# Repeating a constant product on TensorE while it waits, in a fused RWKV-7, GLA and PEER inference step

## The reference, cut to what matters

```python
def _peer(h, wq, subkeys, u, v):
    ...
        q = (xt @ wq).reshape(PEER_BLOCK, PEER_HEADS, 2, PEER_HALF).astype(f32)
        s = jnp.einsum('thpk,hpnk->thpn', q, subkeys.astype(f32))
    ...
        ue = jnp.take(u, expert, axis=0)
        act = jax.nn.gelu(jnp.einsum('thed,td->the', ue, xt).astype(f32), approximate=False)
        ve = jnp.take(v, expert, axis=0)
        return jnp.einsum('the,thed->td', (gate * act).astype(xt.dtype), ve)

for li in range(DEPTH):
    hm = _rmsnorm(x, norm1_g[li]) * (1.0 + sc1) + sh1      # sc, sh, gt from silu(c) @ ada_w
    x = x + gt1 * mix(hm)                                   # RWKV-7 (li = 0) or GLA (li = 1)
    hc = _rmsnorm(x, norm2_g[li]) * (1.0 + sc2) + sh2
    x = x + gt2 * _peer(hc, ...)
```

## Time and profile before

| | |
|---|---|
| time, median of three runs | 3062.83 us (3052.18 to 3067.35) |
| span of the profiled execution | 3042.5 us; the profile gives no other time for it |
| TensorE busy | 1712.4 us (56%), mean granted clock 0.740 |
| VectorE, GpSimd, ScalarE busy | 1595.7, 1320.5, 276.7 us |
| bytes moved by DMA | 828 MB, mean 272 GB/s |

### The profile page before, as it was taken

The page is one execution under the profiler, slowest core; times in us unless marked ns, Lnnn a source line. Parts: engine busy times, 40 slices in busy tenths (PEclk is TensorE's granted clock), DMA queues, the critical chain, the costliest instruction groups (busy, mean ns, idle before and its releaser), DMA issues.

```text
span 3042.5 us, 23984 instructions
## 1 busy us (share of the span) xinstructions
PE 1712.4 (56%) x8811; PEld 1006.3 (33%) x8811; DVE 1595.7 (52%) x2984; ACT 276.7 (9%) x435; POOL 1320.5 (43%) x1160
## 2 busy tenths in 40 slices
PE   3879656826867454636685656358446574002533
PEld 1469412316845113333263225143223261000100
DVE  4253376575844526868313135865775246984033
ACT  1111000010110010010100100011210010000000
POOL 0000012543623555655322354557656125787774
PEclk7889878866879766667677877779677785556875
DMA  7430576964768897777977889879879669799997
GB/s 267 168 125 1 201 280 207 349 220 138 232 221 298 299 325 259 227 239 234 338 284 261 306 286 332 286 264 381 299 277 373 230 225 319 274 332 391 409 409 318
DMA packets 296703, 827.97 MB, mean 272 GB/s; under 512 B 45950, under 2 KB 57134, under 8 KB 296588
## 3 DMA queue, kind: packets, MB, share of 16 engines
q0 software_dynamic: 165888, 604.05, 55.1%
q1 hardware_dynamic: 120132, 218.02, 20.6%
q10 hardware_dynamic: 10568, 4.38, 0.5%
HBM read 816.05 MB, written 10.31 MB: 272 GB/s over the span
## 4 chain that ended last, share of the span: by engine, by line
PE 34%; DVE 22%; DMA 19%; POOL 13%; issue 7%; ACT 3%; PEld 0%; SPq 0%; ACTq 0%; DVEq 0%; PEldq 0%; POOLq 0%
PE psum L1882 31%; POOL arena L695 9%; DMA arena<-in_peer_v,idx_v 6%; DVE arena L1075 6%; DVE arena L1092 6%; POOL wring L695 5%; DMA wring<-in_ada_w 3%; DMA wring<-in_gla_w_in 2%; DMA wring<-in_rw_w_rkv 2%; PE psum L1892 1%; DVE hc L1075 1%; ACT arena L741 1%; DVE hT L1075 1%; DMA vring<-mod_d 1%; DMA wring<-in_peer_v,idx_u 1%
## 5 line engine op out<-in xcount | busy, mean ns | idle before, releaser
L695 POOL DMA_INDIRECT arena<-in_peer_u,idx_u x476 | 628.1, 1320 | 955.7 <-DVEq L1669 415.2
L1882 PE MATMUL psum<-arena 128*32 128x512 f32 (+7 forms) x3666 | 660.2, 619 | 531.3 <-DMA arena<-in_peer_v,idx_v 216.6
L695 POOL DMA_INDIRECT arena<-in_peer_v,idx_v x428 | 431.6, 1008 | 634.6 <-PE psum L1882 477.3
L1092 DVE CUSTOM_DVE_ANT_0 arena<-arena,hc 128x1024 f32<-128x1024 f32 x476 | 565.0, 1225 | 257.9 <-DMA arena<-in_peer_u,idx_u 220.9
L1882 PEld LDWEIGHTS psum<-arena 128*32 128x32 f32 (+2 forms) x3666 | 328.2, 177 | 818.4 <-issue 609.6
L1882 PE MATMUL psum<-wring,arena 128*32 128x512 f32 (+3 forms) x808 | 231.1, 692 | 85.4 <-DMA wring<-in_peer_v,idx_v 43.9
L1882 PE MATMUL psum<-wring,hT 128*128 128x512 f32 (+1 forms) x480 | 192.2, 560 | 27.5 <-DMA wring<-in_gla_w_in 13.6
L1882 PE MATMUL psum<-hT,wring 128*128 128x128 f32 (+4 forms) x1312 | 181.7, 302 | 9.9 <-ACT arena L741 5.0
L1882 PEld LDWEIGHTS psum<-hT,wring 128*128 128x128 f32 (+1 forms) x1312 | 170.9, 203 | 29.7 <-issue 12.9
L741 ACT ACTIVATE arena<-psum 128x512 f32<-128x512 f32 (+6 forms) x125 | 96.7, 774 | 876.8 <-PE psum L1882 644.0
L1882 PEld LDWEIGHTS psum<-wring,arena 128*128 128x128 f32 (+2 forms) x808 | 89.0, 171 | 218.5 <-issue 198.3
(11 more groups left out here) (222 smaller groups left out, 1790.1 us busy)
## 6 DMA issues: line engine op xcount, KB each, us to landing
wring<-in_ada_w SPq DMA_DIRECT2D x24, 2048.0 KB
wring<-in_peer_wq SPq DMA_DIRECT2D x20, 2048.0 KB
wring<-in_rw_w_rkv SPq DMA_DIRECT2D x12, 2048.0 KB
wring<-in_gla_w_in SPq DMA_DIRECT2D x12, 2048.0 KB
wring<-in_rw_wo SPq DMA_DIRECT2D x6, 2048.0 KB
vring<-mod_d SPq DMA_DIRECT2D x22, 512.0 KB
wring<-in_gla_wo SPq DMA_DIRECT2D x4, 2048.0 KB
arena<-in_peer_u,idx_u POOLq DMA_INDIRECT x476, 6.1
```

The source lines that it names most:

```text
L695: pool.indirect_dma_start(slot(s, n), None, v_rows if side else u_rows, bass.IndirectOffsetOnAxis(index, 0)).then_inc(rows_landed[s], 16)
L1092: dve.tensor_tensor_reduce(slot(s, n), slot(s, n), hc[:, t, :], 1.0, 0.0, MUL, ADD, acts[:, (3 * li + t) % 2, col:col + 1]).then_inc(rows_ ...
L1882: return nc.tensor.matmul(out, lhsT, rhs, start=start, stop=stop)
```

## The change

TensorE gets a helper that waits until the next single ScalarE bank is drained and then multiplies `ident` by the 512 columns of `pick` into it, n times; nobody reads the result. It is called with fixed counts at many places of TensorE's program: behind every round of `rest_values` and of the two loops in `out`, ahead of turns, levels, states and weights. A new semaphore `clock_due` lets it start inside `core(1)` before the operands of the turn are there. The queries of the sample tile alone are computed over all 128 columns of its copies.

```diff
@@ class Banks
+    def peek(self):
+        pairs = ((4, 5), (6, 7)) if self.two else ((4, 5),)
+        lanes = [b for pair in zip(*pairs) for b in pair]
+        b = lanes[self.lane % len(lanes)]
+        return b, self.last.get(b, 0)
@@ vector, core
                 tt(aT, aT, up, MUL)
                 serve()
+                if t == 1:
+                    dve.sem_inc(clock_due, 1)
                 tt(r, r, up, MUL)
@@ tensor
             def rest_values():
                 for _ in range(stream.rest()):
                     value_round()
+                    raise_clock(5)
...
+            def raise_clock(n):
+
+                first, earlier = banks.peek()
+                if earlier:
+                    pe.wait_ge(scalar_drained, earlier)
+                for _ in range(n):
+                    mm(psum[:, first * 512:first * 512 + 512], ident[:], pick[:].rearrange("p j n -> p (j n)"))
@@ tensor, core
+                if t == 1:
+                    pe.wait_ge(clock_due, w.next(clock_due))
+                    raise_clock(8)
                 pe.wait_ge(operand_written, w.next(operand_written))
...
                             attention(b)
+                            raise_clock(8)
                             operands()
...
                             attention(b)
+                        raise_clock(3)
...
                     attention(b)
+                    raise_clock(10)
                     operands()
                     level(b)
...
                     for q in range(4):
+                        raise_clock(4 if q else 1)
                         pe.wait_ge(s0_loaded, w.next(s0_loaded, 32))
...
                     for q in range(PAIRS):
+                        raise_clock(3 if q else 6)
                         operands()
@@ tensor, gla_mixer
                 if tiles[0]:
                     sum_lanes()
+                raise_clock(24)
                 h_turned(tiles)
@@ tensor, out
                 scalar_copies()
+                raise_clock({(0, 0): 6, (0, SAMPLE): 6, (1, 1): 5}.get((li, tiles[0]), 0))
                 held = [weight(), weight()]
...
+                raise_clock(36 if li and tiles[0] == 0 else 12)
                 h_turned(tiles)
...
-                                rows = hq[:, k, :] if n > 1 else hT[:, tiles[0], k, 0:cols]
-                                last = mm(ps[:, i * wide:i * wide + cols], wring[:, b, k, i * P:(i + 1) * P], rows, k == 0, k == KD - 1)
+                                rows = hq[:, k, :] if n > 1 else hT[:, tiles[0], k, :]
+                                last = mm(ps[:, i * wide:i * wide + max(cols, P)], wring[:, b, k, i * P:(i + 1) * P], rows, k == 0, k == KD - 1)
...
                             value_round()
+                            raise_clock(5)
@@ tensor, main order
             modulation()
+            raise_clock(20)
             h_turned((0, 1, SAMPLE))
             mix((0,))
             core(0)
             out(0, (0,))
+            raise_clock(14)
             mix((1, SAMPLE))
```

More of the change, by code:

```diff
@@ L297, in program @@
         total_ready = sem("total_ready")
+        clock_due = sem("clock_due")
         total_taken = sem("total_taken")
```

## The result

The changed kernel is slower: 3096.95 us at the median (3077.56 to 3101.03, five runs) against 3058.03 us (3052.18 to 3067.35, five runs), ratio 1.0122 with a 95% interval from 1.0089 to 1.0155. On 3058 us that is +37 us, from +27 to +47. Forecast were +18 us and 3081 us. Three single executions of later kernels (3237, 3636 and 5119 us) stand far apart from the rest of theirs and are in none of the ratios.

A forecast was written before the change was run, and what follows sets the result against it. No engine bounds the kernel throughout; TensorE has 34% of the chain. Value rounds +47, other overruns +19 and gains -48 make +18 us on the 3062.8 us median: 3081 us, range 3020 to 3106.

The forecast's parts named there:

- The end: Last value rounds: with five repetitions each takes 6.37 us, more than the 5.12 between rounds; +47 us, bounds +30 and +52.
- The first slot groups' rounds: About 20 value rounds of the first layer's first tile, with two slot groups: high clock and five repetitions give -7 us.
- Ten rounds of the second layer: Value rounds with two slot groups: a gain of 3 us is taken back by repetitions behind two earlier rounds; 0.
- The queries: The sample's four query blocks: 128 columns instead of 32 shorten 56.5 us to 41.5; -15 us, bounds -9 and -17.
- Three ahead of 210.86: First core: three repetitions fill 2.67 of 2.96 us of idle, so the 13 us behind no longer start low; -4.6 us.
- `clock_due`: Turn at 667.34 in core(1): eight repetitions make it 4 to 5 us late, turn and deal 1.8 faster; +2.8 us.
- the gain in the cores: Halves of tile 1's core, waits partly filled: -7.8 us behind 745.03, -3.5 of a possible 8.9 behind 703.38.
- Rival (b): Clock falls again in waits left partly open; only queries, 210.86 and 745.03 pay; +39 us, 3102 us, chance .15.
- The last turn: Second layer's last turn of hc, at 2436.30: no idle ahead, so twelve repetitions less a faster turn cost +10.3 us.
- The 36 at the second layer's first turn: 36 repetitions take 32.0 us in 24.78 of idle; after gains at the high clock, +2.6 us.
- The sample's core: Four repetitions ahead of each state load, and the products behind them: -2 us a half, -4 us in all.
- The mean clock: TensorE's mean granted clock over the whole kernel should rise from 0.74 to above 0.9.

The follow-up runs named there:

- no_end: The changed kernel without repetitions in the value rounds of the last prompt tile and the sample tile at the end; ratio to the kernel before 0.9990.
- best kernel: fitted with 11 instead of 8 repetitions in each half of tile 1's core, and other waits filled with more repetitions too; ratio to the kernel before 0.9824.
- queries_alone: The kernel before with the sample's queries over all 128 columns and no repetition anywhere; ratio to the kernel before 0.9916.
- fitted: The changed kernel without the end's repetitions and with counts elsewhere cut to what each wait holds, none at the last turn; ratio to the kernel before 0.9886.
- end_three_alone: The kernel before with three repetitions behind each value round of the last prompt tile and the sample tile at the end; ratio to before 0.9992.

## Why the prediction was right in sign and short in size

**Right.** A repetition costs its full price: (6.34 - 1.85) / 5 = 0.90 us at the high clock, 0.89 forecast. The end goes over the 5.12 us of DMA: forecast +47, measured 44.6 to 49.0 in two traces and +43 by ratio. The first slot groups' rounds: forecast -7, measured -7 to -8 in the changed kernel and no_end. Ten rounds of the second layer: 0 forecast; the stretch from 2485 to 2770 has -3.1 and -0.7, against -4.8 to 0 in kernels with none (and up to +12.7 in one kernel with five, so it could not show a few us). The queries: forecast -15, measured -14. Three ahead of 210.86: -4.6 and -4.4. `clock_due`: +2.8, and +3.4 and +2.9. Most of the sum stood on terms that hold, and the sign came from the largest of them.

**The step that failed** is the gain in the cores: "Eight ahead of 745.03 leave 1.9 us of the 9.00 open; the products behind its twin at 703.38 run 13.6 us without a pause at 1.2 GHz, about half of it goes: -7.8", and -3.5 for 703.38. Together 11.3 were forecast, and three kernels with these counts gained 1.7, -0.6 and 2.6. That is about half of the 19 us by which the sum was short. I treated idle time as fixed in proportion: most of a wait filled, most of the gain had. The runs show that at this place it is close to all or nothing. With 3.3 and 2.1 us open at most 2.6 us were won, with 0.7 or less 14.3 us, three more than I had put in for a partly filled wait. Rival (b) gave this as its reason, "where a wait stays partly open, nothing may be won", and its time, +39 us, is nearest to the +37 measured. That it is so near is partly luck: it kept the 7.8 at 745.03, against its own reason, which did not come, and took away the 7 of the rounds, which did. I had given it .15; the row for it was in the earlier trace rows, the clock low through 13.6 us of unbroken work after a wait of 10 us, and I priced that row only as a possible size and not as a mechanism.

**Terms that were mis-sized.** The last turn, +10.3 forecast, measured +15.9 and +12.7: I gave back 0.4 for a faster turn, and counted twelve repetitions at the full clock, where in the changed kernel they took 11.58 us and not 10.7. Some 3 us more are the loss of clock in the short waits behind the turn, which five of the twelve kernels without repetitions there have too, so the change can't be charged with them. The 36 at the second layer's first turn, +2.6 forecast, +4.1 and +7.3 measured; 25 there gain up to 4. The sample's core, -4 forecast, nothing found. The mean clock, above 0.9 forecast, 0.836 measured: partly the same error, since waits left partly open were followed by low stretches; how much of it, no run shows. The missed terms lie almost all on one side, so it is the size of the largest, right one that made the sign hold.

**What the mean clock told.** I used the mean of 0.740 against the page TensorE: Matmul & The Clock Gate of the Trainium skill, Part 1, by which the penalty of the ramp is under 1% of a span. The best kernel here raises the mean only to 0.818 and stands 0.9% under queries_alone (0.9916 less 0.9824), 28 us, with some 0.3% of uncertainty on each side. That is within the page's size. But the wide queries, a further 0.8%, gain by the clock as well, and together the best kernel is 1.8% under the one before, 54 us, with low stretches left. So for this kernel the page's size is too small, as I objected, but the mean was a poor measure of how much: it counts stretches in which TensorE waits or is off the chain with the same weight as those that cost time.

**Not settled.** fitted is 1.0%, 32 us, under no_end, and the three places sum to 24. The three are 3 us at `clock_due`, 11 at the turn that was at 1859 and 10 at the last. The traces of the changed kernel and no_end, whose programs are alike up to 2770, stand 19 us apart there, and only some of that is placed (landing times in the sample's core, above). The stretch from 293 to 655, -7.4 in the changed kernel, is +0.6 in no_end and -5.0 in end_three_alone, which has no repetition there: it can't be credited to the change.

## What to carry to other kernels

A repetition that keeps TensorE busy is free up to the moment when its operand is due and costs its full 0.9 us beyond; so read the idle time at each place and give each its own count, and give none where the timeline shows no idle time. If the purpose is the clock, a wait that is filled in part may bring nothing: here eight brought at most 2.6 us and eleven 14, and the line between them differs from place to place, so look at the price of the products behind the wait and not at the share that is filled. Look at narrow products as well: 32 columns cost as much as 128 at the high clock, and let it fall. Where DMA sets a pace, compare the round and its filling with that pace, not with the idle time of one round: at the end five a round cost 1.4% and three nothing, with the 5.12 us of DMA between them.

## What the runs showed of the hardware that was not expected

- Products of 64 columns behind 1.56 to 3.28 us of idle time ran at the high clock for 0 to 2.3 us and then took 0.64 us a pair instead of 0.39, for as long as they lasted (some 11 us); behind 1.27 and 0.70 us all of them ran at 0.39.
- Products of 32 columns lost the high clock after 3.9 us of unbroken work and went from 0.11 to 0.20 us an instruction; in their place products of 128 columns, 0.115 us each, kept it.
- The same four waits of 0.63 to 1.27 us, at one place of the program and with no repetition near them, kept the clock in seven traces and lost it in five.
- A product repeated on the same operands costs 0.90 us, no less than one with new weights.
- With TensorE busy 128 of 140 us beside it, DMA moved the same 409 GB/s as with 70: the repetitions take nothing from the gathers.
- The landing of a state written to memory at the same point of the program took 8.87 us in one kernel and 13.36 in another; single executions of one kernel go from 3040.52 to 3069.67 us, so places were compared over several traces.
